# A mixture-of-experts decoder block whose expert weights arrive in 2 MB transfers of 16 KB pieces

## The chip, the cores and the metric

The kernel runs on one core of a Trainium2 chip. The metric is the device time of one execution in microseconds. Three runs of the kernel before took 1349.27, 1349.53 and 1350.82 us; the median is 1349.53 us. The profiled execution took 1348.86 us.

## The reference

The block has a mixing part and an expert part, all in float32, on 256 tokens of width 1024:

```
h = x + hybrid_mixer(rms_norm(x), ...)            # RWKV-7, windowed attention, memory attention, gates
logits = rms_norm(h) @ w_router + b_router        # 32 experts
gates  = softmax(top 4 of logits)
for each expert e, for the tokens that chose it:
    u = xn[tok] @ w1[e] + b1[e]                    # w1[e]: 1024 x 2048, 8 MB
    a = clamped_swiglu(u)                          # u[::2] and u[1::2] -> 1024 columns
    y = a @ w2[e] + b2[e]                          # w2[e]: 1024 x 1024, 4 MB
    h[tok] += gate * y
out = rms_norm(h)
```

All 32 experts are read from HBM once, 12 MB each, 384 MB together. A sum over the contraction rows of w1 (the 1024 columns of xn) or of w2 (the 1024 columns of a) can be taken in any order of the rows, as long as the left factor is laid out in the same order.

## The kernel before, in words

The program has one instruction stream per engine and is synchronised by semaphores. SP issues nearly all DMAs; PE multiplies; DVE and ACT do the pointwise work.

**Mixer part.** 42 chunks of weights of up to 1 MB (`order` in `mixer_chunks`) are loaded through the same ring as the experts' weights. The ring has 16 slots of 8 KB per partition, 1 MB each: slots 0 to 5 lie side by side in `ring`, slots 6 to 15 at the places that `WIDE_AT` lists, in areas that the mixer's own tiles hold before.

**Expert part.** An expert takes 12 chunks: 8 of w1 (128 rows of 2048 columns, one row of 8 KB per partition) and 4 of w2 (256 rows of 1024 columns, two rows of 4 KB per partition, 128 rows apart). The chunks go round the ring in the order w1(0), w1(1), w2(0), w1(2), w2(1), and so on. `load_w1` and `load_w2` (L417 and L425) wait until the chunk that held the slot has been used, `slots_used`, a counter which PE raises once for each chunk; each slot has a semaphore `slot_full` for the landing. Before the w1 of an expert SP also issues two loads of its bias row (L414): 2 partitions by 4 KB each. The first group of experts and the last are written out, those between run in loops.

PE works on pairs of experts (`pair`): `up` of the even expert (8 chunks, 4 matmuls each), `down` of the expert before (4 chunks, 4 matmuls each), `turn` (4 transposes of the activation), `up` of the odd expert with the scatter of the last pair between its chunks, the gather of the next pair's tokens, `down` of the even expert, `turn`. The tokens of an expert sit in 64 places. All of these matmuls stand in the profile as L460, the helper that issues them, each one as two instructions: a chunk is x8.

DVE adds the bias and does the clamped SwiGLU (L1646 to L1659); `act_` is its result, which PE turns into `actT` for `down`. `hn` is the normalised residual (L1586), the left factor of the router and of w1.

Of the kernel before, what the change touches and what calls it, by code (L numbers as in the profile page):

```python
# [16 lines left out]
P = 128  # L17
D = 1024
T = 256
KC = D // P  # L20
# [3 lines left out]
ALU = mybir.AluOpType  # L24
# [7 lines left out]
LEVELS = 6  # L32
# [11 lines left out]
NE = 32  # L44
# [6 lines left out]
RING = 16  # L51
NARROW = 6
SLOT = 2048
CPE = 12
GROUP = 4
TURNS = GROUP * CPE // RING

WIDE_AT = (88, 96, 8, 72, 80, 0, 16, 24, 32, 40)

# [80 lines left out]
def build(nc, x, mem, w_in, rwkv_w2, rwkv_a2, rwkv_g2, swa_sinks, w_mem_kv, w_gate, w_branch, w_out,  # L140
          ffn_norm_w, w_router, b_router, w_exp1, b_exp1, w_exp2, b_exp2, final_norm_w, params, consts, out):
    order, slots = mixer_chunks()
    NMIX = len(order)
# [7 lines left out]
    with ExitStack() as ctx:  # L151
# [10 lines left out]
        xrows = sb("xrows", [P, TT, D])  # L162
# [119 lines left out]
        def slot(s):  # L282
            return ring[:, s * SLOT:(s + 1) * SLOT] if s < NARROW else kb(WIDE_AT[s - NARROW], 8)


        slot_full = [sem(f"slot_full{s}") for s in range(RING)]
# [65 lines left out]
        def _(sp):  # L352
# [7 lines left out]
            for n, (name, c) in enumerate(order):  # L360
                s = slots[n]
                if previous[n] is not None:
                    sp.wait_ge(slots_used, previous[n] + 1)
                elif s == NARROW:
                    sp.wait_ge(pv_sb, 4)
                elif s == NARROW + 2:
                    sp.wait_ge(xx_ps, 2 * (LEVELS - 1))
                elif s == NARROW + 3:
                    sp.wait_ge(y_ps, NCH)
                elif s == NARROW + 5:  # L370
                    sp.wait_ge(y_rwkv_sb, TT)
# [26 lines left out]
            sp.dma_start(b2rows[0:NE, :], b_exp2[0]).then_inc(late_loaded, 16)  # L398
            sp.dma_start(wrt, w_router[0].rearrange("(c p) e -> p c e", p=P)).then_inc(late_loaded, 16)
            sp.dma_start(brt[:], b_router.to_broadcast([P, NE])).then_inc(late_loaded, 16)  # L400

            def load_w1(q, a, r, zero=False, bias=True):

                g = q * (NE // GROUP) + a
                for c in range(KC):
                    s, _, n = w1_place(c, g, r, zero)
                    if c == 0 and bias:
                        sp.wait_ge(b1_spread, g * GROUP + (r - 1))
                        sp.sem_inc(b1_due, 1)
                    sp.wait_ge(slots_used, n + (NMIX - RING + 1))  # L410
                    if c == 0 and bias:
                        for twice in range(2):
                            at = 32 * twice
                            sp.dma_start(b1rows[at:at + 65:64, r % 2, :],  # L414
                                         b_exp1[0, bass.ds(a * GROUP + r, 1), :].rearrange("a (h f) -> (a h) f", h=2))\
                              .then_inc(b1_full[r % 2], 16)
                    sp.dma_start(slot(s), w_exp1[0, bass.ds(a * GROUP + r, 1), c * P:(c + 1) * P, :].rearrange("a p f -> p (a f)"))\  # L417
                      .then_inc(slot_full[s], 16)

            def load_w2(q, a, r, final=False):  # L420
                g = q * (NE // GROUP) + a
                for i in range(4):
                    s, _, n = w2_place(i, g, r, final)
                    sp.wait_ge(slots_used, n + (NMIX - RING + 1))
                    sp.dma_start(slot(s).rearrange("p (c f) -> p c f", c=2),  # L425
                                 w_exp2[0, bass.ds(a * GROUP + r, 1), 2 * i * P:(2 * i + 2) * P, :].rearrange("a (c p) f -> p (a c) f", p=P))\
                      .then_inc(slot_full[s], 16)

# [29 lines left out]
        def _(pe):  # L458
# [407 lines left out]
            for t in range(TT):  # L866
                if t == 1:
                    turn_input(1)
                for c in range(KC):
                    if c % 4 == 0:  # L870
                        pe.wait_ge(hnT_sb, 2 * t + c // 4 + 1)
                    if t == 0 and c == 0:
                        pe.wait_ge(late_loaded, 16 * 5)
                        pe.wait_ge(resid, 1)
# [23 lines left out]
            def up(g, r, E, N, parity, between, zero=False):  # L898

                for c in range(KC):  # L900
                    s, times, n = w1_place(c, g, r, zero)
                    if parity == 0 and c % 4 == 0:
                        pe.wait_ge(xg_sb, N * 2 + c // 4 + 1)
                    pe.wait_ge(slot_full[s], times * 16 + 16 * uses[s])
                    for z in range(2):
# [8 lines left out]

            def down(g, r, E, final=False):

                pe.wait_ge(actT_sb, E + 1)
                for i in range(4):
                    s, times, n = w2_place(i, g, r, final)
                    pe.wait_ge(slot_full[s], times * 16 + 16 * uses[s])  # L920
                    for cc in range(2):
# [46 lines left out]
            def pair(q, a, p, first, last, turn_wait=None):  # L968
# [7 lines left out]
                if not first:  # L976
                    down(g, r - 1, E - 1)
                if very_first:
# [20 lines left out]
                if not last:  # L999
                    gather(N + 1)  # L1000
                down(g, r, E)
                turn(E + 1)

            def one_pass(q, very_first=False):
# [12 lines left out]
                turn_gates(N0 + NPAIR - 1, False)  # L1017
                down(q * (NE // GROUP) + a, GROUP - 1, q * NE + NE - 1, True)
                scatter(N0 + NPAIR - 1, 0)
# [296 lines left out]
        def _(dve):  # L1316
# [259 lines left out]
            for t in range(TT):  # L1576
# [4 lines left out]
                if t == 0:  # L1581
                    dve.wait_ge(late_loaded, 16 * 5)
                link(dve.reciprocal(ss[:, 4 + t:5 + t], ss[:, 4 + t:5 + t]))
                for b in range(2):
                    half = slice(b * 512, (b + 1) * 512)
                    STT(hn[:, t, half], xrows[:, t, half], ss[:, 4 + t:5 + t], ffnw[:, half], ALU.mult, ALU.mult).then_inc(hn_sb, 1)  # L1586

# [53 lines left out]
            def swiglu(E, very_first=False):  # L1641
# [15 lines left out]
                if not very_first:  # L1657
                    dve.wait_ge(actT_ps, E)
                TTn(act_, lin, sig, ALU.mult).then_inc(act_sb, 1)  # L1659

# [90 lines left out]
```

## Time and profile before

| what | value |
|---|---|
| median of three runs | 1349.53 us |
| profiled execution | 1348.86 us |
| its span (first to last instruction) | 1347.1 us |
| PE busy | 1236.4 us, 92% |
| PE weight loads busy | 592.8 us, 44% |
| DVE, ACT busy | 338.3 us, 199.1 us |
| read from HBM | 447.99 MB |
| PE granted clock, mean | 0.987 |

The span starts 1348.86 - 1347.1 = 1.8 us short of the whole time. PE's busy time counts pipelined matmuls up to a modelled end, so that a high share does not say that PE is at its peak; whether PE or a transfer sets the pace has to be read from what PE waits for. The share of the DMA engines can read a little above 1.

### The profile page before, as it was taken

The numbers are of one execution on the slowest core, as the hardware profiler recorded it, in microseconds if no ns is written. First come the engines' busy times: TensorE is split into PE (matmuls) and PEld (weight loads), VectorE is DVE, ScalarE is ACT, GpSimd is POOL, SyncE is SP. The second block draws the span as 40 slices with busy tenths as digits, with TensorE's granted clock in tenths as the row PEclk, the third lists the DMA queues.
The fourth block names the chain that finished last, engine by engine and source line by source line (L and its number), as shares of the span: only waits on it lengthen the run. The fifth ranks groups of instructions, "written<-read, shape, count | busy, mean of one in ns | idle before, by whom it ended". The sixth has DMA issues, their size and how long they took to land.

```text
span 1347.1 us, 16403 instructions
## 1 busy us (share of the span) xinstructions
PE 1236.4 (92%) x6534; PEld 592.8 (44%) x6534; DVE 338.3 (25%) x574; ACT 199.1 (15%) x381; POOL 0.2 (0%) x4
## 2 busy tenths in 40 slices
PE   7999989999989999999998989898998989898985
PEld 6886778888453333333332323232332323232321
DVE  1156463211122123122221212122221212121122
ACT  1225422100111011110111101010110111010112
POOL 0000000000000000000000000000000000000000
PEclk9999989999989999999999999999999999999998
DMA  9343102694549999999999999999999999999992
GB/s 346 110 155 122 64 3 65 225 396 144 206 176 402 417 417 416 417 416 416 417 417 418 418 418 418 417 417 416 418 417 417 418 418 418 416 415 415 413 416 103
DMA packets 95357, 449.72 MB, mean 334 GB/s; under 512 B 8624, under 2 KB 21040, under 8 KB 62544
## 3 DMA queue, kind: packets, MB, share of 16 engines
q1 hardware_dynamic: 95008, 447.99, 83.2%
q10 hardware_dynamic: 304, 1.08, 0.3%
q8 instruction: 34, 0.56, 0.2%
q14 instruction: 11, 0.09, 0.0%
HBM read 447.99 MB, written 1.05 MB: 333 GB/s over the span
## 4 chain that ended last, share of the span: by engine, by line
PE 43%; SPq 32%; DMA 17%; DVE 4%; issue 3%; ACT 1%; ACTq 0%; PEldq 0%; DVEq 0%
PE ps L460 41%; SPq L425 17%; DMA upper<-in_w_exp 9%; SPq L417 7%; DMA ring<-in_w_exp 7%; SPq L414 7%; DVE ring L1381 0%; DVE upper L1472 0%; PE ps L695 0%; SPq L410 0%; DMA xrows<-in_x 0%; PE ps L933 0%; ACT ring L1133 0%; PE ps L476 0%; ACTq L1237 0%
## 5 line engine op out<-in xcount | busy, mean ns | idle before, releaser
L460 PE MATMUL ps<-ring,upper 128*64 128x512 f32 (+4 forms) x2928 | 585.1, 538 | 46.4 <-DMA ring<-in_w_exp 40.5
L460 PEld LDWEIGHTS ps<-ring,upper 128*64 128x64 f32 (+2 forms) x2928 | 176.7, 138 | 405.3 <-issue 289.1
L460 PE MATMUL ps<-upper 128*64 128x512 f32 (+6 forms) x1592 | 278.8, 443 | 24.6 <-DMA upper<-in_w_exp 16.1
L460 PEld LDWEIGHTS ps<-upper 128*64 128x64 f32 (+4 forms) x1592 | 135.1, 162 | 169.7 <-issue 109.3
L460 PE MATMUL ps<-xT,ring 128*128 128x256 f32 x640 | 142.8, 381 | 0.0
L460 PEld LDWEIGHTS ps<-xT,ring 128*128 128x128 f32 x640 | 120.5, 190 | 17.6 <-issue 1.3
L1646 DVE TENSOR_TENSOR upper<-ps,upper 128x512 f32<-128x512 f32 x32 | 22.1, 692 | 364.1 <-PEq L913 364.1
L1666 DVE TENSOR_TENSOR xrows<-xrows,ps 128x1024 f32<-128x1024 f32 x32 | 39.1, 1222 | 264.5 <-PE ps L460 264.5
L1256 ACT ACTIVATE upper<-upper 128x512 f32<-128x512 f32 x32 | 20.2, 631 | 566.1 <-DVE upper L1649 566.1
L1262 ACT ACTIVATE factors<-ps 64x512 f32<-64x512 f32 x64 | 37.9, 593 | 211.8 <-PEq L928 211.1
L460 PE MATMUL ps<-factors,upper 128*128 128x512 f32 x128 | 63.2, 617 | 1.5 <-ACT factors L1262 1.5
L460 PE MATMUL ps<-upper,ring 128*128 128x256 f32 (+1 forms) x304 | 63.5, 367 | 0.0
L460 PEld LDWEIGHTS ps<-upper,ring 128*128 128x128 f32 (+1 forms) x304 | 51.3, 191 | 9.4 <-issue 3.0
L1639 DVE STREAM_SHUFFLE upper<-merged 128x1024 f32<-128x1024 f32 x32 | 42.2, 1320 | 0.2
L460 PEld LDWEIGHTS ps<-factors,upper 128*128 128x128 f32 x128 | 21.8, 189 | 43.7 <-issue 43.7
L933 PEld LDWEIGHTS ps<-cst,upper 128*128 128x128 f32 x128 | 13.7, 143 | 36.7 <-issue 35.1
L933 PE MATMUL ps<-cst,upper 128*128 128x128 f32 x128 | 21.1, 289 | 8.9 <-PE ps L460 8.0
L460 PE MATMUL ps<-xT,upper 128*128 128x256 f32 x128 | 28.3, 379 | 0.0
L460 PE MATMUL ps<-ring,merged 128*128 128x512 f32 x64 | 27.8, 592 | 0.0
L460 PEld LDWEIGHTS ps<-xT,upper 128*128 128x128 f32 x128 | 24.3, 190 | 3.3
L1639 DVE LOAD_MASK_SELECT upper<-merged x32 | 0.4, 14 | 92.6 <-DMA merged<-in_b_exp 92.6
L1510 DVE TENSOR_TENSOR upper<-upper,ps 128x512 f32<-128x512 f32 x8 | 5.5, 688 | 72.3 <-PE ps L460 72.3
(210 smaller groups left out, 499.9 us busy)
## 6 DMA issues: line engine op xcount, KB each, us to landing
ring<-in_w_exp SPq DMA_DIRECT2D x288, 1024.0 KB, 21.4
upper<-in_w_exp SPq DMA_DIRECT2D x96, 1024.0 KB, 22.5
ring<-in_w_gate SPq DMA_DIRECT2D x8, 1024.0 KB, 5.0
ring<-in_w_in SPq DMA_DIRECT2D x8, 896.0 KB, 11.2
ring<-in_w_branch SPq DMA_DIRECT2D x6, 1024.0 KB, 5.3
ring<-in_w_in SPq DMA_DIRECT2D x8, 640.0 KB, 3.9
ring<-in_w_mem_kv SPq DMA_DIRECT2D x4, 1024.0 KB, 4.9
upper<-in_w_gate SPq DMA_DIRECT2D x4, 1024.0 KB, 11.0
```

Of the source, the lines that this page charges most:

```text
L414: sp.dma_start(b1rows[at:at + 65:64, r % 2, :], b_exp1[0, bass.ds(a * GROUP + r, 1), :].rearrange("a (h f) -> (a h) f", h=2))\
L417: sp.dma_start(slot(s), w_exp1[0, bass.ds(a * GROUP + r, 1), c * P:(c + 1) * P, :].rearrange("a p f -> p (a f)"))\
L425: sp.dma_start(slot(s).rearrange("p (c f) -> p c f", c=2), w_exp2[0, bass.ds(a * GROUP + r, 1), 2 * i * P:(2 * i + 2) * P, :].rearrange("a ...
L460: return pe.matmul(o, l, r, start=start, stop=stop, skip_group_check=True)
L933: last = pe.transpose(ps[:, 2, m * P:(m + 1) * P], act_[:, m * P:(m + 1) * P], ident)
L1256: act.activation(sig, glu, ACT.Sigmoid, scale=ALPHA).then_inc(sig_sb, 1)
L1262: act.activation(yrow[64 * parity:64 * parity + 64, dh * 512:(dh + 1) * 512], ps[64 * dh:64 * dh + 64, 3, :], ACT.Copy).then_inc(yrow_sb, 1)
L1510: link(TTn(gsig[:, m % 2, :], gsig[:, m % 2, :], ps[:, 7, :], ALU.mult))
L1639: dve.stream_shuffle(b1all, b1rows[:, parity, :], [0] * 32).then_inc(b1_spread, 1)
L1646: TTn(glu, ps[:, 0, :], b1all[:, 0:D:2], ALU.add).then_inc(glu_raw, 1)
L1666: TTn(a, a, ps[:, bank:bank + 2, :], ALU.add).then_inc(acc_sb, 1)
```

## The change

The contraction rows are permuted within blocks of 512: partition p of a block now holds rows 4p to 4p+3, where it held rows p, p+128, p+256 and p+384. Four neighbouring rows of w2 are then 16 KB in one piece, and so are two neighbouring rows of w1. Two ring slots that lie side by side are filled by one transfer of 2 MB: 128 partitions, one piece of 16 KB each. For w1 the pieces start 32 KB apart (the other two rows of the four belong to the next transfer), for w2 16 KB apart. SP waits until both chunks that held the two slots have been used; PE waits for a landing only at every second chunk. The four last chunks, w2 of expert 31, still come one by one, now in pieces of 8 KB.

The left factors take the same order: `hn` is written with its columns regrouped (which makes router and w1 agree), `act_` likewise for w2; the router's weights come in two DMAs in the same order. `WIDE_AT` is reordered so that slots 6 and 7, 8 and 9, ... are neighbours; with that the mixer's chunks in slots 8 to 11 lie in other places and two waits of the mixer's loads move.

```diff
-WIDE_AT = (88, 96, 8, 72, 80, 0, 16, 24, 32, 40)
+WIDE_AT = (88, 96, 72, 80, 0, 8, 16, 24, 32, 40)
...
+        def twin_slot(s):
+            return ring[:, s * SLOT:(s + 2) * SLOT] if s < NARROW else kb(WIDE_AT[s - NARROW], 16)
...
                 elif s == NARROW + 2:
-                    sp.wait_ge(xx_ps, 2 * (LEVELS - 1))
-                elif s == NARROW + 3:
                     sp.wait_ge(y_ps, NCH)
-                elif s == NARROW + 5:
+                elif s == NARROW + 6:
                     sp.wait_ge(y_rwkv_sb, TT)
...
-            sp.dma_start(wrt, w_router[0].rearrange("(c p) e -> p c e", p=P)).then_inc(late_loaded, 16)
+            for b in range(2):
+                sp.dma_start(wrt[:, 4 * b:4 * b + 4, :], w_router[0, b * 512:(b + 1) * 512, :].rearrange("(p c) e -> p c e", c=4)).then_inc(late_loaded, 16)
...
-                for c in range(KC):
+                for c in range(0, KC, 2):
                     s, _, n = w1_place(c, g, r, zero)
...
-                    sp.wait_ge(slots_used, n + (NMIX - RING + 1))
+                    sp.wait_ge(slots_used, n + (NMIX - RING + 2))
...
-                    sp.dma_start(slot(s), w_exp1[0, bass.ds(a * GROUP + r, 1), c * P:(c + 1) * P, :].rearrange("a p f -> p (a f)"))\
+                    b, j = c // 4, c % 4
+                    sp.dma_start(twin_slot(s), w_exp1[0, bass.ds(a * GROUP + r, 1), b * 512:(b + 1) * 512, :]
+                                 .rearrange("a (p c) f -> p a c f", c=4)[:, :, j:j + 2, :].rearrange("p a c f -> p (a c f)"))\
...
-                for i in range(4):
+                for i in range(0, 4, 1 if final else 2):
                     s, _, n = w2_place(i, g, r, final)
...
+                    if final:
+                        sp.dma_start(slot(s), src[:, :, j:j + 2, :].rearrange("p a c f -> p (a c f)")).then_inc(slot_full[s], 16)
+                    else:
+                        sp.dma_start(twin_slot(s), src.rearrange("p a c f -> p (a c f)")).then_inc(slot_full[s], 16)
...
             def up(g, r, E, N, parity, between, zero=False):
-                    pe.wait_ge(slot_full[s], times * 16 + 16 * uses[s])
+                    if c % 2 == 0:
+                        pe.wait_ge(slot_full[s], times * 16 + 16 * uses[s])
...
-                    STT(hn[:, t, half], xrows[:, t, half], ss[:, 4 + t:5 + t], ffnw[:, half], ALU.mult, ALU.mult).then_inc(hn_sb, 1)
+                    STT(hn[:, t, half].rearrange("p (c q) -> p q c", c=4), xrows[:, t, half].rearrange("p (q c) -> p q c", c=4),
+                        ss[:, 4 + t:5 + t], ffnw[:, half].rearrange("p (q c) -> p q c", c=4), ALU.mult, ALU.mult).then_inc(hn_sb, 1)
...
-                TTn(act_, lin, sig, ALU.mult).then_inc(act_sb, 1)
+                TTn(act_.rearrange("p (c q) -> p q c", c=4), lin.rearrange("p (q c) -> p q c", c=4), sig.rearrange("p (q c) -> p q c", c=4),
+                    ALU.mult).then_inc(act_sb, 1)
```

On SP, where the mixer's last loads have been issued and the experts' begin, 6 + 2 + 1 + 2 + 5 loads of w1 and four of w2 stood before (L417 is w1, L425 w2; 128x2048 is one row of 8 KB per partition):

```order
L417 DMA ring<-in_w_exp 128x2048 [waits slots_used] x6
L417 DMA upper<-in_w_exp 128x2048 [waits slots_used] x2
L417 DMA ring<-in_w_exp 128x2048 [waits slots_used]
L417 DMA upper<-in_w_exp 128x2048 [waits slots_used] x2
L417 DMA ring<-in_w_exp 128x2048 [waits slots_used] x5
L425 DMA ring<-in_w_exp 128x2x1024 [waits slots_used] x4
```

The same stretch of SP after the change (L420 is w1, L434 w2):

```order
L420 DMA ring<-in_w_exp 128x4096 [waits slots_used] x3
L420 DMA upper<-in_w_exp 128x4096 [waits slots_used] x2
L420 DMA ring<-in_w_exp 128x4096 [waits slots_used] x3
L434 DMA ring<-in_w_exp 128x4096 [waits slots_used] x2
```

Half as many loads stand there, each of 4096 elements per partition, and each waits for two chunks instead of one.

On PE, near the end, `down` of expert 30 stood before as four chunks with a wait for a landing each:

```order
L460 MATMUL ps<-ring,upper 64x512 [waits slots_used,slot_full8,actT_sb]
L460 MATMUL ps<-ring,upper 64x512 x3
L460 MATMUL ps<-upper 64x512 [waits slot_full9]
L460 MATMUL ps<-upper 64x512 x3
L460 MATMUL ps<-upper 64x512 [waits slot_full10]
L460 MATMUL ps<-upper 64x512 x3
L460 MATMUL ps<-ring,upper 64x512 [waits slot_full11]
L460 MATMUL ps<-ring,upper 64x512 x3
```

The same stretch of PE now:

```order
L467 MATMUL ps<-upper 64x512 [waits slots_used,slot_full8,actT_sb]
L467 MATMUL ps<-upper 64x512 x7
L467 MATMUL ps<-ring,upper 64x512 [waits slot_full10]
L467 MATMUL ps<-ring,upper 64x512 x7
```

The first of two chunks can start only when both have landed; `down` of expert 31 behind it keeps its four waits.

## Rows read from the trace of the kernel before

**Rows 1.** The page's 40 slices of the span: DMA share in tenths, and GB/s

```profile
DMA  9343102694549999999999999999999999999992
GB/s 346 110 155 122 64 3 65 225 396 144 206 176 402 417 417 416 417 416 416 417 417 418 418 418 418 417 417 416 418 417 417 418 418 418 416 415 415 413 416 103
```

**Rows 2.** Timeline of SP's queue: start us, us, issues; two bias loads, four experts apart

```profile
1025.51 5.11 SPq L414 DMA_DIRECT2D merged<-in_b_exp  x2
...
1147.78 5.11 SPq L414 DMA_DIRECT2D merged<-in_b_exp  x2
```

**Rows 3.** Timeline of PE, one up and down: start us, us, instructions, idle before

```profile
1086.96 2.02 PE L460 MATMUL ps<-ring,upper 128*64 128x512 f32 x8 [0.46 <-DMA ring<-in_w_exp]
1089.44 2.02 PE L460 MATMUL ps<-ring,upper 128*64 128x512 f32 x8 [0.46 <-DMA ring<-in_w_exp]
1091.92 2.02 PE L460 MATMUL ps<-ring,upper 128*64 128x512 f32 x8 [0.46 <-DMA ring<-in_w_exp]
1094.46 2.02 PE L460 MATMUL ps<-ring,upper 128*64 128x512 f32 x8 [0.52 <-DMA ring<-in_w_exp]
1097.03 1.94 PE L460 MATMUL ps<-ring,upper 128*64 128x512 f32 x8 [0.54 <-DMA ring<-in_w_exp]
1099.59 1.94 PE L460 MATMUL ps<-ring,upper 128*64 128x512 f32 x8 [0.62 <-DMA ring<-in_w_exp]
1102.15 1.94 PE L460 MATMUL ps<-upper 128*64 128x512 f32 x8 [0.63 <-DMA upper<-in_w_exp]
1104.76 1.94 PE L460 MATMUL ps<-upper 128*64 128x512 f32 x8 [0.67 <-DMA upper<-in_w_exp]
```

**Rows 4.** Busy time by stretch: stretch us, PE, PEld, DVE, ACT, POOL, clock, DMA share, GB/s

```profile
640.00:701.10 61.10, 55.71 (x251) 19.23 (x251) 13.83 (x24) 6.30 (x11) 0.00 (x0) 1.00 1.02 417
...
1026.00:1034.00 8.00, 6.70 (x28) 1.78 (x30) 0.00 (x0) 0.00 (x0) 0.00 (x0) 1.00 1.02 411
1044.00:1054.00 10.00, 9.12 (x40) 2.71 (x37) 1.33 (x2) 2.16 (x4) 0.00 (x0) 1.00 1.01 423
```

**Rows 5.** The page's DMA packets, and its queues: packets, MB, share

```profile
DMA packets 95357, 449.72 MB, mean 334 GB/s; under 512 B 8624, under 2 KB 21040, under 8 KB 62544
...
q8 instruction: 34, 0.56, 0.2%
```

**Rows 6.** Timeline where the experts begin: SP's last prefetch, PE's first chunks, SP's restart

```profile
366.50 0.33 SPq L417 DMA_DIRECT2D ring<-in_w_exp  x1
...
386.08 4.27 PE L460 MATMUL ps<-ring,upper 128*64 128x512 f32 x18 [0.69 <-ACT upper L1252]
...
388.14 2.18 SPq L425 DMA_DIRECT2D ring<-in_w_exp  x2
```

**Rows 7.** Busy time by stretch, after the restart

```profile
388.00:440.00 52.00, 50.30 (x228) 18.60 (x226) 12.65 (x21) 6.38 (x10) 0.00 (x0) 0.97 0.98 389
```

**Rows 8.** Busy time by stretch, at the end of the transfers

```profile
1318.00:1322.00 4.00, 2.78 (x14) 1.12 (x14) 0.00 (x0) 1.42 (x3) 0.00 (x0) 1.00 0.24 96
1322.00:1326.00 4.00, 3.59 (x18) 1.23 (x20) 0.00 (x0) 2.12 (x4) 0.00 (x0) 1.00 0.12 50
```

**Rows 9.** Timeline of PE at the end

```profile
1318.45 1.94 PE L460 MATMUL ps<-ring,upper 128*64 128x512 f32 x8 [0.58 <-DMA ring<-in_w_exp]
...
1322.41 5.37 PE L460 MATMUL ps<-ring,upper 128*64 128x512 f32 x24 [1.02 <-ACT upper L1267]
...
1328.33 1.94 PE L460 MATMUL ps<-ring,upper 128*64 128x512 f32 x8 [0.55 <-DMA ring<-in_w_exp]
```

**Rows 10.** DVE's two changed instructions: ns min/median/max, first and last start us

```profile
L1586 DVE SCALAR_TENSOR_TENSOR upper<-xrows,ss,xT x4: 744/748/752, 356.0 to 370.0; 128x512 f32<-128x512 f32 x4
...
L1659 DVE TENSOR_TENSOR upper<-upper x32: 691/692/693, 403.7 to 1313.8; 128x512 f32<-128x512 f32 x32
```

**Rows 11.** Busy time by stretch: the input projection's weights, 7 KB pieces 12 KB apart

```profile
16.00:20.00 4.00, 4.00 (x20) 3.54 (x19) 1.22 (x3) 2.48 (x5) 0.00 (x0) 1.00 1.04 385
...
24.00:30.00 6.00, 6.00 (x29) 5.30 (x28) 0.00 (x0) 0.00 (x0) 0.00 (x0) 1.00 1.02 417
```

More of the change, by code:

```diff
@@ L421, in load_w2 @@
                 g = q * (NE // GROUP) + a
-                for i in range(4):
+                for i in range(0, 4, 1 if final else 2):
                     s, _, n = w2_place(i, g, r, final)
[L424 to L427, printed above, removed]
+                    sp.wait_ge(slots_used, n + (NMIX - RING + (1 if final else 2)))
+                    b, j = i // 2, 2 * (i % 2)
+                    src = w_exp2[0, bass.ds(a * GROUP + r, 1), b * 512:(b + 1) * 512, :].rearrange("a (p c) f -> p a c f", c=4)
+                    if final:
+                        sp.dma_start(slot(s), src[:, :, j:j + 2, :].rearrange("p a c f -> p (a c f)")).then_inc(slot_full[s], 16)
+                    else:
+                        sp.dma_start(twin_slot(s), src.rearrange("p a c f -> p (a c f)")).then_inc(slot_full[s], 16)
             def load_group(q, a, count=GROUP, bias_from=0):
@@ L872, in _ @@
                     if t == 0 and c == 0:
-                        pe.wait_ge(late_loaded, 16 * 5)
+                        pe.wait_ge(late_loaded, 16 * 6)
                         pe.wait_ge(resid, 1)
@@ L913, in up, with down @@
                 pe.sem_inc(up_ps, 1)
-            def down(g, r, E, final=False):
+            def down(q, g, r, E, final=False):
                 pe.wait_ge(actT_sb, E + 1)
@@ L919, in down @@
                     s, times, n = w2_place(i, g, r, final)
-                    pe.wait_ge(slot_full[s], times * 16 + 16 * uses[s])
+                    if i % 2 == 0:
+                        pe.wait_ge(slot_full[s], times * 16 + 16 * uses[s])
+                    elif final:
+                        pe.wait_ge(slot_full[s], q * 16 + 16 * (uses[s] + 1))
                     for cc in range(2):
@@ L976, in pair @@
                 if not first:
-                    down(g, r - 1, E - 1)
+                    down(q, g, r - 1, E - 1)
                 if very_first:
@@ L1000, in pair @@
                     gather(N + 1)
-                down(g, r, E)
+                down(q, g, r, E)
                 turn(E + 1)
@@ L1017, in one_pass @@
                 turn_gates(N0 + NPAIR - 1, False)
-                down(q * (NE // GROUP) + a, GROUP - 1, q * NE + NE - 1, True)
+                down(q, q * (NE // GROUP) + a, GROUP - 1, q * NE + NE - 1, True)
                 scatter(N0 + NPAIR - 1, 0)
@@ L1581, in _ @@
                 if t == 0:
-                    dve.wait_ge(late_loaded, 16 * 5)
+                    dve.wait_ge(late_loaded, 16 * 6)
                 link(dve.reciprocal(ss[:, 4 + t:5 + t], ss[:, 4 + t:5 + t]))
```

## The prediction

> **What bounds the kernel now.** I began with the page's slices [rows 1]. From the twelfth of 40 on the DMA engines are busy nearly all the time and move 402 to 418 GB/s; only the last slice falls off. That is the expert part, some 940 of the 1347 us. PE reads 9 in most of these slices too, so the slices alone do not decide. The first row of the stretches, one pair of experts, does [rows 4]: 61.10 us, of which PE is busy 55.71, with the clock at 1.00, so 5.4 us a pair are left over, and the DMA share is 1.02. What ends PE's idle time stands in its timeline [rows 3]: each chunk of eight instructions takes 2 us and is preceded by half a microsecond of waiting for a DMA into ring or upper. PE follows the landings one by one. The period of an expert is read from SP's bias loads, which come once each: (1147.78 - 1025.51) / 4 = 30.57 us [rows 2].
>
> The same rows say what a landing costs. While w1 lands (8 KB pieces) the steps are 2.48, 2.48 and 2.54 us, mean 2.50; while w2 lands (4 KB pieces) they are (1104.76 - 1094.46) / 4 = 2.575 us [rows 3]. Eight of the one and four of the other make 30.3 us; the 0.27 us to the period are the two bias loads, whose four 4 KB pieces lie on two partitions and so on few engines.
>
> That the pace is set by the engines with the most work, not by the mean rate, is seen at the end: the traffic falls to 96 GB/s between 1318 and 1322 us and 50 between 1322 and 1326 [rows 8], while PE still waits for a landing at 1328.33 [rows 9]. Most engines are done ten microseconds before the last. Thirty experts with 0.27 to 0.3 us more on a few engines make just about that lead. So I count with PE's landing steps, not with the 417 GB/s.
>
> **The pieces.** 128 pieces over 16 engines are 8 each for a w1 chunk, 256 are 16 each for a w2 chunk; the bytes are equal. Eight pieces more cost 2.575 - 2.50 = 0.075 us, which is 9.4 ns a piece. The mean rates agree: 423 GB/s in a stretch of 8 KB pieces and 411 in one of 4 KB [rows 4] are 2.48 and 2.55 us for 1 MB. Two w1 chunks take 5.00 us with 16 pieces an engine; in one transfer with 8 pieces they take 5.00 - 0.075 = 4.925 us, and two w2 chunks the same, instead of 5.15. This assumes that a 16 KB piece travels as one. The trace has packets of that size: 34 on the instruction queue with 0.56 MB together, 16.5 KB each [rows 5]. And the 8 KB pieces are not cut: 95357 packets less the 62544 under 8 KB leave 32813, where w1 alone makes 32 x 8 x 128 = 32768.
>
> The sum: 16 of the 384 chunks are in the ring before PE begins. From the restart at 388.14 us [rows 6] 240 chunks of w1 and 128 of w2 follow: 240 x 2.50 + 128 x 2.575 + 30 x 0.27 = 937.7 us; the trace has 1328.33 - 388.14 = 940.2, the rest being the first landing's delay. After: 182 transfers x 4.925 + 4 single chunks x 2.50 + 30 x 0.27 = 914.5 us. That is -23.2 us.
>
> The bounds: the closest steps (2.54 and 2.56) give 2.5 ns a piece, a transfer of 4.98 us and -13 us; the farthest (2.48 and 2.61) give 16 ns, 4.83 us and -41 us. I take the means, which the rates bear out.
>
> **The coarser ring.** Three costs.
> At the restart the first transfer needs two used chunks. SP's queue stood still between 366.50 and 388.14, when PE had used the first [rows 6]; PE goes at 4.27 us for 18 instructions, 1.9 us for the eight of a chunk. The restart moves back by 1.9 us, and since the transfers set the end from there, all of it counts. Behind it, DMA is just kept fed for a while (389 GB/s between 388 and 440 us, [rows 7]); releases in pairs add a bit of idle, which I put at 0.4 us: four transfers end some 20 us after the restart, just where PE has come through the first two chunks of the second expert. Bounds 0 and 2.
> Later PE needs (61.10 - 5.4) / 2 = 27.9 us for an expert and the transfers 29.8, so DMA remains the slower side. Of eight double slots one or two are with PE and six are ordered ahead; nothing starves.
> At the end PE used the last chunk of expert 30 from 1318.45 on, and began expert 31's `down` at 1322.41, 4.0 us later (two of matmuls, two of transposes and evictions) [rows 9]. Now both last chunks of expert 30 land together, four single landings (9.9 us) before the last. PE needs 3.9 us for them, 2.0 for the transposes, and 5.37 / 3 = 1.8 us for each of four chunks: 13.1 us, so it ends 3.2 us after the last landing, where it ended 1.94 after it. +1.3 us, with PE the bound there; bounds 0 and 2.
> Together +3.6 us.
>
> **What is put at nothing.** DVE's 32 writes of `act_` (0.69 us each, [rows 10]) now go in four interleaved columns; a doubled time would hide, since DVE waits most of an expert's 30 us and even the last one ends at 1314.5, six microseconds before PE transposes it. The four writes of `hn` are different: PE waits for them before the router. Two lie on the path; equal elements, so I take 0, with twice their 0.75 us, +1.5, as the upper bound. SP issues half as many loads and stands in its queue anyway. The router's second DMA is issued during the mixer. The mixer's loads that change place wait for things that the neighbouring load already waited for, and the queue did not stand there.
>
> Sum: -23.2 + 3.6 = -19.6 us against the profiled 1348.86: 1329.3. The median of the runs is 0.7 above the profiled one, so 1330.0.
>
> **Rivals.**
> A, the pieces are cut at 8 KB. Then w1 gains nothing and w2 0.075 us a chunk: 128 x 0.075 = -9.6 us, with the costs of the ring -6.0: 1343.5. Against it: packets of 16 KB exist; for it: those belong to another queue and none of a load is above 8 KB. The Trainium skill (DMA: Bandwidth & Descriptors, SWDGE vs HWDGE vs iDMA) says a packet has preferably at most 4096 bytes, for descriptors written by software; by that rule 4 and 8 KB pieces would cost the same and the change would be left with its costs, +3.6 us or 1353. The trace disagrees, with its 32813 packets of 8 KB or more.
> B, slower: w1's pieces now start 32 KB apart and the engines read from places 128 KB apart, instead of through one unbroken megabyte; if HBM serves that worse, each w1 transfer pays. The nearest rows read 7 KB pieces 12 KB apart: 417 GB/s in one stretch, 385 in another, where small loads are mixed in [rows 11]. If 401, the middle of these, were due to the steps, a w1 transfer would take 5.00 x 422 / 401 = 5.26 us, 0.335 more than counted, and 120 of them +40: about 1370. The gain is gone when a w1 transfer takes 19.6 / 120 = 0.16 us more than 4.925, that is from 5.09 us. Against it: 417 is what pieces of that size would give in any place. The Trainium skill (DMA: Bandwidth & Descriptors, Latency and other measured facts) has copies at a row step of 512 KB almost at full rate and at 2 MB and above down to three quarters and half; no run here shows such steps, and 32 KB is far below, so it adds no chance.
> C, the ring's costs eat the gain: pieces cost 2.5 ns only, and the upper bounds of the ring (1.9 + 2 + 2 + 1.5) hold: -13 + 7.4, 1344.
> D, the pieces cost more than the means say, at 16 ns: -41 + 3.6, 1312.
>
> **Chances.** Forecast 0.65, A 0.12, B 0.12, C 0.06, D 0.05. The range that holds eight in ten is 1317 to 1345: it reaches most of the way to D and includes A and C, and leaves out B. A difference below 0.2%, 2.7 us, can hardly be told from none. Faster 0.85, same 0.04, slower 0.11.
>
> **What would show it.** SP's bias loads in the profile after should come every 29.8 us (30.2 under A, over 30.6 under B); PE should wait for a DMA at every second chunk of eight, with steps of 4.93 us in both w1 and w2; the mean rate should be near 427 GB/s; the page should count some 40,700 packets fewer in all (65,536 of the experts' weights become 190 x 128 + 4 x 128 = 24,832) and about as many of 8 KB or more as that last number. The first expert load after the prefetch should be issued at about 390.0 us, and PE should run 13 us without a wait at the end. Equal steps for w1 and w2 at 5.0 would speak for A; w1's above w2's for B. A restart much later than 390 us, or idle DMA in the middle of the loop, would show that I have the ring wrong.

## The result and the profile after

The changed kernel takes 1331.72 us (median of four runs, 1330.19 to 1332.04) against 1350.09 before on the same chip: ratio 0.9862, interval 0.9845 to 0.9879, or 18.4 us faster. Forecast were 1330.0 and a range of 1317 to 1345. Run again beside later kernels it gave 1331.72 once more. Its profiled execution has a span of 1328.8 us, 18.3 less than before.

The page's slices, which answer to [rows 1], show the same plateau, higher and shorter:

```profile
DMA  9343101694449999999999999999999999999991
GB/s 347 106 163 127 64 3 62 200 395 177 158 158 400 417 427 428 428 426 428 429 428 429 427 428 428 428 428 427 429 428 428 427 428 428 428 428 427 427 424 71
DMA packets 50861, 449.70 MB, mean 338 GB/s; under 512 B 4577, under 2 KB 17249, under 8 KB 25985
```

428 GB/s stand where 417 stood. Of 8 KB or more there are 50861 - 25985 = 24876 packets, and 24832 were forecast: the 16 KB pieces travel whole. Cut at 8 KB they would be twice as many. In all 44,500 packets are gone, not 40,700, since the small packets fell too (under 512 B: 8624 to 4577).

SP's timeline, start us, us, issues, at the bias loads, against [rows 2]:

```profile
1029.88 1.11 SPq L416 DMA_DIRECT2D merged<-in_b_exp  x2
...
1149.33 1.11 SPq L416 DMA_DIRECT2D merged<-in_b_exp  x2
```

Four experts in 119.45 us: the period is 29.86 us, 0.71 less than 30.57 (forecast 29.82).

PE's timeline in the loop, against [rows 3]:

```profile
1080.80 3.82 PE L467 MATMUL ps<-ring,upper 128*64 128x512 f32 x16 [1.07 <-DMA ring<-in_w_exp]
1085.69 3.65 PE L467 MATMUL ps<-ring,upper 128*64 128x512 f32 x16 [1.07 <-DMA ring<-in_w_exp]
1090.63 3.65 PE L467 MATMUL ps<-upper 128*64 128x512 f32 x16 [1.28 <-DMA upper<-in_w_exp]
...
1135.69 3.82 PE L467 MATMUL ps<-upper 128*64 128x512 f32 x16 [0.23 <-DMA upper<-in_w_exp]
1140.51 3.82 PE L467 MATMUL ps<-ring,upper 128*64 128x512 f32 x16 [0.99 <-DMA ring<-in_w_exp]
```

PE now takes two chunks at a landing and waits a microsecond for the next. The first two steps end in landings of w2 (the rows of 3.65 us) and are 4.89 and 4.94 us; the last ends in one of w1 (3.82 us) and is 4.82 us. Forecast was 4.93 for both.

Where the transfers start again after the prefetch (against [rows 6, 7]), SP's timeline, and then the busy time by stretch, whose last two columns are DMA share and GB/s:

```profile
389.76 3.93 SPq L434 DMA_DIRECT2D ring<-in_w_exp  x2
```

```profile
388.00:440.00 52.00, 49.96 (x224) 18.40 (x222) 13.38 (x21) 6.38 (x10) 0.00 (x0) 0.97 0.93 374
```

The restart is at 389.76 us (forecast 390.0, before 388.14), and 374 GB/s instead of 389 move until 440.

PE's timeline at the end (against [rows 9]):

```profile
1295.45 3.65 PE L467 MATMUL ps<-upper 128*64 128x512 f32 x16 [0.31 <-PE ps L467]
1299.58 3.65 PE L467 MATMUL ps<-ring,upper 128*64 128x512 f32 x16 [0.47 <-DMA ring<-in_w_exp]
...
1305.25 7.09 PE L467 MATMUL ps<-ring,upper 128*64 128x512 f32 x32 [1.02 <-ACT upper L1278]
```

The last wait for a landing is 0.47 us at 1299.58; the four chunks of expert 31 run through in 7.09 us without one. PE ends them at 1312.34 where it ended at 1330.27. But PE was nearly without waits before that, too: of what it waited for between 1274 and 1313 us, the profile's waits (engine and line, waited for, us, times, longest) give

```profile
PE ps L467 <- DMA ring<-in_w_exp: 1.9, 3, 1.0
```

One thing was put at nothing and is not. The changed lines of DVE, against [rows 10], each from its own line's view:

```profile
L1671 DVE TENSOR_TENSOR upper<-upper x32: 1034/1064/1078, 403.5 to 1298.0; 128x512 f32<-128x512 f32 x32
```

```profile
L1597 DVE SCALAR_TENSOR_TENSOR upper<-xrows,ss,xT x4: 1094/1094/1108, 355.2 to 369.5; 128x512 f32<-128x512 f32 x4
```

Writing the 512 elements in four interleaved columns takes 1.06 and 1.09 us instead of 0.69 and 0.75.

### The profile page after: what moved, and what is told of

It reads as the page before. It is cut to its first block, busy times and chain, and to the rows that moved or that the text cites. A ratio compares the mean times of both kernels' runs of the same rounds, so it can differ in the third digit from the quotient of the medians.

```text
span 1328.8 us, 15782 instructions
## 1 busy us (share of the span) xinstructions
PE 1222.1 (92%) x6534; PEld 599.7 (45%) x6534; DVE 350.4 (26%) x574; ACT 199.0 (15%) x381; POOL 0.2 (0%) x4
## 2 busy tenths in 40 slices
DMA packets 50861, 449.70 MB, mean 338 GB/s; under 512 B 4577, under 2 KB 17249, under 8 KB 25985
## 4 chain that ended last, share of the span: by engine, by line
PE 62%; DMA 30%; DVE 4%; ACT 1%; issue 1%; SPq 0%; PEldq 0%; DVEq 0%
PE ps L467 61%; DMA ring<-in_w_exp 30%; DVE ring L1392 0%; PE ps L944 0%; DVE upper L1483 0%; PE ps L702 0%; DMA xrows<-in_x 0%; ACT ring L1144 0%; PE ps L483 0%; ACT factors L1273 0%; DVE upper L1597 0%; PE ps L852 0%; PE ps L611 0%; DVE ring L1389 0%; ACT ring L1170 0%
## 5 line engine op out<-in xcount | busy, mean ns | idle before, releaser
L467 PE MATMUL ps<-ring,upper 128*64 128x512 f32 (+4 forms) x2928 | 572.4, 534 | 45.5 <-DMA ring<-in_w_exp 41.1
L467 PE MATMUL ps<-upper 128*64 128x512 f32 (+6 forms) x1624 | 283.4, 442 | 20.9 <-DMA upper<-in_w_exp 12.2
L467 PEld LDWEIGHTS ps<-upper 128*64 128x64 f32 (+3 forms) x1624 | 144.3, 163 | 151.7 <-issue 132.6
L467 PE MATMUL ps<-xT,ring 128*128 128x256 f32 x672 | 150.0, 381 | 0.0
L467 PEld LDWEIGHTS ps<-xT,ring 128*128 128x128 f32 x672 | 126.7, 190 | 18.4 <-issue 1.3
L467 PE MATMUL ps<-upper,ring 128*128 128x256 f32 (+1 forms) x272 | 56.6, 368 | 0.0
L467 PEld LDWEIGHTS ps<-upper,ring 128*128 128x128 f32 (+1 forms) x272 | 45.5, 192 | 8.7 <-issue 3.0
L467 PEld LDWEIGHTS ps<-factors,upper 128*128 128x128 f32 x128 | 21.8, 189 | 43.7 <-issue 43.7
L1671 DVE TENSOR_TENSOR upper<-upper 128x512 f32<-128x512 f32 x32 | 34.1, 1064 | 1.2 <-ACT upper L1267 0.2
L1263 ACT ACTIVATE upper<-ps 128x512 f32<-128x512 f32 x32 | 17.4, 595 | 34.5 <-PE ps L467 34.5
L1666 DVE SCALAR_TENSOR_TENSOR upper<-upper 128x512 f32<-128x512 f32 x32 | 22.2, 693 | 1.1
## 6 DMA issues: line engine op xcount, KB each, us to landing
ring<-in_w_out SPq DMA_DIRECT2D x4, 1024.0 KB, 14.3
```

The costliest lines, as they stand in the source:

```text
L467: return pe.matmul(o, l, r, start=start, stop=stop, skip_group_check=True)
L1263: act.activation(xg[:, 4 * b:4 * b + 4, :], ps[:, 4 + b, :].rearrange("p (c s) -> p c s", c=4), ACT.Copy).then_inc(xg_sb, 1)
L1666: STT(lin, lin, 1.0, glu, ALU.add, ALU.mult).then_inc(prod_sb, 1)
L1671: TTn(act_.rearrange("p (c q) -> p q c", c=4), lin.rearrange("p (q c) -> p q c", c=4), sig.rearrange("p (q c) -> p q c", c=4), ALU.mult).t ...
```

## The experiments

### Pieces of 8 KB, single slots, permuted rows

```diff
-                for c in range(0, KC, 2):
+                for c in range(KC):
...
-                    sp.wait_ge(slots_used, n + (NMIX - RING + 2))
+                    sp.wait_ge(slots_used, n + (NMIX - RING + 1))
...
-                    sp.dma_start(twin_slot(s), ...[:, :, j:j + 2, :]...)
+                    sp.dma_start(slot(s), ...[:, :, j:j + 1, :]...)
```

(w2 likewise as four loads, and PE waits at each chunk.)

> Rows permuted as in the changed kernel, but each slot filled by its own 1 MB transfer with one 8 KB piece per partition: w1 in 8 KB pieces 32 KB apart, w2 in 8 KB pieces instead of 4 KB, 16 single slots. My theory (a piece costs about 9.4 ns beyond its bytes, their distance nothing): w1 lands every 2.50 us as before, w2 every 2.50 instead of 2.575, so 128 chunks x 0.075 = 9.6 us less than before, no cost of a coarser ring, some 1 us for the wider writes of DVE on the way to the experts: 0.994 of before, 1341 us. Rival 1 (the size of a transfer brings the gain, not the piece): no change, 1350. Rival 2 (pieces 32 KB apart are read more slowly, and the 16 KB pieces only hide that): w1 above 2.50 us, 1350 or more.

1343.25 us, ratio 0.9952 (0.9939 to 0.9966): 6.6 us less than before (1349.85 beside it), where 8.6 were expected. Transfers are as large as before, so their size is not what brings these 6.6 us; rival 1 falls. The timeline of PE, in w1 and after it in w2:

```profile
1083.68 2.02 PE L467 MATMUL ps<-ring,upper 128*64 128x512 f32 x8 [0.42 <-DMA ring<-in_w_exp]
1086.16 2.02 PE L467 MATMUL ps<-ring,upper 128*64 128x512 f32 x8 [0.46 <-DMA ring<-in_w_exp]
...
1096.09 1.94 PE L467 MATMUL ps<-ring,upper 128*64 128x512 f32 x8 [0.54 <-DMA ring<-in_w_exp]
1098.57 1.94 PE L467 MATMUL ps<-upper 128*64 128x512 f32 x8 [0.54 <-DMA upper<-in_w_exp]
```

Both land every 2.48 us. w1's pieces now lie 32 KB apart and cost what they cost side by side; rival 2 falls, and with it rival B of the prediction. The expert's period is (1137.12 - 1015.99) / 4 = 30.28 us by SP's bias loads. That is 0.29 less than before, 8.9 us over the 30.67 experts (368 chunks) that land after the restart; why only 6.6 came of it is not shown.

### Double slots with the old rows, and each layer alone: a square of four

The changed kernel with both, one or none of the layers in the new row order; rings, waits and 2 MB transfers the same. Old rows in w1 read

```diff
-                    sp.dma_start(twin_slot(s), w_exp1[...b * 512:(b + 1) * 512, :]
-                                 .rearrange("a (p c) f -> p a c f", c=4)[:, :, j:j + 2, :]...)
+                    sp.dma_start(twin_slot(s).rearrange("p (c f) -> p c f", c=2),
+                                 w_exp1[...c * P:(c + 2) * P, :].rearrange("a (c p) f -> p (a c) f", p=P))
```

> 2 MB transfers into double slots, but the rows in their old order: w1 in 8 KB pieces, w2 in 4 KB pieces, so the piece count of before with the transfers and the ring of after. My theory: the landings cost as before (5.00 and 5.15 us per 2 MB), and only the ring's costs show, 1.9 us at the restart, up to 2 of idle DMA behind it, 1.3 at the end: 3.6 to 5 us slower than before, 1.003. Rival (a transfer has a cost of its own, so fewer of them bring the gain): as fast as the changed kernel, 0.986.

> 2 MB transfers into double slots; only w2 in the new row order with 16 KB pieces, w1 in its old order with two 8 KB pieces. My theory: against the kernel with old rows and double slots, 62 transfers land in 4.925 instead of 5.15 us and four chunks in 2.50 instead of 2.575: 14.3 us less, so some 10 us faster than before, 0.9925. If pieces cost nothing beyond 8 KB, 62 x 0.15 = 9.6 us less.

> 2 MB transfers into double slots; only w1 in the new row order with 16 KB pieces, w2 in its old order with four 4 KB pieces. My theory: against the kernel with old rows and double slots, 120 transfers land in 4.925 instead of 5.00 us: 9 us less, some 5 us faster than before, 0.996. The gains of this and of the kernel with w2 alone should add up to that of the changed kernel over the one with old rows and double slots. If pieces cost nothing beyond 8 KB: no difference to old rows with double slots.

| double slots, 2 MB transfers | median us | ratio to before (interval) | expert's period us |
|---|---|---|---|
| old rows in both (8 KB and 4 KB) | 1352.50 | 1.0019 (1.0010 to 1.0028) | 30.54 |
| w1 in 16 KB pieces | 1344.45 | 0.9959 (0.9946 to 0.9973) | 30.24 |
| w2 in 16 KB pieces | 1339.81 | 0.9927 (0.9914 to 0.9941) | 30.15 |
| both (the changed kernel) | 1331.72 | 0.9862 (0.9845 to 0.9879) | 29.86 |

Larger transfers alone are 2.6 us slower. The rows of w1 bring 8.1 us and those of w2 12.7, together 20.8; from 1352.50 to 1331.72 it is 20.8. They add up; that they do so to a tenth is luck, since the runs of the w1 kernel alone lie between 1342.61 and 1345.53. So within a microsecond or two nothing but the number of pieces is needed to tell the story. The forecasts of the two were 9 and 14.3.

One rival stands in no forecast: SP's own queue. Before the change the issue of two bias loads took 5.11 us [rows 2], after it 1.11, and SP's queue has a large share of the chain of work that ended last. The chain by engine, from the pages of the kernel before, of the one with w2 alone in 16 KB pieces, and of the changed kernel:

```profile
PE 43%; SPq 32%; DMA 17%; DVE 4%; issue 3%; ACT 1%; ACTq 0%; PEldq 0%; DVEq 0%
...
PE 60%; DMA 33%; DVE 4%; ACT 1%; issue 1%; ACTq 0%; SPq 0%; PEldq 0%; DVEq 0%
...
PE 62%; DMA 30%; DVE 4%; ACT 1%; issue 1%; SPq 0%; PEldq 0%; DVEq 0%
```

SP's queue is out of the chain in the second kernel already, and yet it is 8.1 us slower than the changed kernel. So w1's share of the gain is not SP's. For w2's share there is no such pair of runs; against SP as the limit speaks that the DMA engines had work all the time before, with a share of 1.01 to 1.02 [rows 4], and that a piece costs nearly the same in both layers: by the periods (30.54 - 30.24) / 32 = 9.4 ns for w1, which has 32 pieces an engine fewer, and (30.54 - 30.15) / 48 = 8.1 ns for w2, which has 48 fewer.

### Bias pieces of 32 bytes

```diff
-                            sp.dma_start(b1rows[at:at + 65:64, r % 2, :],
-                                         b_exp1[...].rearrange("a (h f) -> (a h) f", h=2))
+                            sp.dma_start(b1rows[at:at + 65:64, r % 2, 0:8],
+                                         b_exp1[...].rearrange("a (h f) -> (a h) f", h=2)[:, 0:8])
```

> The changed kernel, whose bias loads of experts 2 to 31 bring only the first 8 numbers of each half (pieces of 32 bytes instead of 4 KB); the rest of their bias row is left as it was. My theory: the pace is that of the few DMA engines that carry the bias pieces beside their share of the weights; with those gone the period of an expert falls from 29.87 us to that of the others, about 0.3 us less, 30 experts 8 to 9 us: 1323, and the last traffic of all engines ends within 2 us instead of trailing for 10. Rival (the mean rate of 428 GB/s is the bound, the trailing engines are a harmless end effect): 8 KB less an expert is 0.02 us, no change, 1331.

1321.69 us, ratio 0.9786 (0.9773 to 0.9799): 10.0 us less than the changed kernel, with a plateau of 428 GB/s as there. It leaves out most of 30 bias rows, so it serves to measure only. The busy time by stretch (DMA share and GB/s at the end of a row) at the end of the transfers, the changed kernel first:

```profile
1284.00:1296.00 12.00, 11.69 (x48) 3.51 (x48) 3.13 (x4) 0.00 (x0) 0.00 (x0) 1.00 0.99 415
1296.00:1300.00 4.00, 3.53 (x18) 1.14 (x16) 3.68 (x7) 0.63 (x1) 0.00 (x0) 1.00 0.39 164
1300.00:1304.00 4.00, 3.84 (x22) 1.50 (x18) 0.00 (x0) 0.60 (x2) 0.00 (x0) 1.00 0.19 78
1304.00:1308.00 4.00, 2.98 (x17) 1.04 (x16) 0.00 (x0) 2.94 (x5) 0.00 (x0) 1.00 0.07 29
1308.00:1309.00 1.00, 1.00 (x8) 0.31 (x6) 0.00 (x0) 0.00 (x0) 0.00 (x0) 1.00 0.04 16
```

and with short bias pieces:

```profile
1284.00:1296.00 12.00, 10.45 (x50) 3.41 (x46) 4.39 (x8) 1.48 (x3) 0.00 (x0) 1.00 1.01 424
1296.00:1300.00 4.00, 2.99 (x14) 1.06 (x16) 0.00 (x0) 2.69 (x5) 0.00 (x0) 1.00 0.64 268
1300.00:1304.00 4.00, 4.00 (x20) 1.15 (x16) 0.00 (x0) 0.00 (x0) 0.00 (x0) 1.00 0.01 4
```

Without the bias pieces all engines end together; with them a few trail for ten microseconds: a share of 0.19 is about three engines of 16, one of 0.07 about one. The expert's period is (1142.47 - 1025.05) / 4 = 29.36 us: 16 KB of bias pieces an expert, a thousandth of its bytes, cost 0.51 us of 29.86. The prediction had 0.27.

Thirty experts at 0.51 would make 15.3 us, and the time fell by 10.0. SP's bias loads, in the changed kernel and then in this one, show why the rest is missing:

```profile
431.00 1.03 SPq L416 DMA_DIRECT2D merged<-in_b_exp  x2
...
647.35 1.11 SPq L416 DMA_DIRECT2D merged<-in_b_exp  x2
```

```profile
433.00 1.03 SPq L416 DMA_DIRECT2D merged<-in_b_exp  x2
...
649.46 0.52 SPq L416 DMA_DIRECT2D merged<-in_b_exp  x1
```

Eight experts take 216.35 and 216.46 us, 27.05 us each, and in neither kernel does PE wait for a DMA in that stretch. PE lives on the full ring there and sets the pace, and the bias pieces cost nothing. Only the 20 or so experts after it pay, at 0.51 us each.

This puts the landing steps right, if the bias pieces cost 0.51 us in the other kernels too, which was measured in the changed one alone. Less 0.51, an expert's period is 30.06 before, 29.77 in the first experiment and 29.35 after. The first experiment has only 8 KB pieces: 29.77 / 12 = 2.481 us for 1 MB. Then w2's 4 KB pieces took (30.06 - 8 x 2.481) / 4 = 2.553 and the 16 KB pieces take 29.35 / 12 = 2.446. Eight pieces less on an engine save 0.072 us from 4 to 8 KB; from 8 to 16 KB four less save 0.035 us. Both are 9 ns a piece. The differences of the periods need no term for the bias and say the same: (30.57 - 30.28) / 32 = 9.1 ns and (30.28 - 29.86) / 48 = 8.8 ns.

### DVE writes in unbroken order

```diff
-                    STT(hn[:, t, half].rearrange("p (c q) -> p q c", c=4), xrows[:, t, half].rearrange(...),
+                    STT(hn[:, t, half], xrows[:, t, half], ss[:, 4 + t:5 + t], ffnw[:, half], ALU.mult, ALU.mult)
...
-                TTn(act_.rearrange("p (c q) -> p q c", c=4), lin.rearrange(...), sig.rearrange(...), ALU.mult)
+                TTn(act_, lin, sig, ALU.mult)
```

> The changed kernel with DVE's writes of hn and act_ in unbroken order as before, so that the left factors do not fit the order of the weights' rows (the products are of permuted rows; all sizes and all work are the same). My theory: the writes in four interleaved columns took 1064 and 1016 ns instead of 692 and 706, and of that only the two halves of hn in front of the router and the first expert's act_ are waited for: 0.9 to 1.4 us less than the changed kernel, 1330.5. Rival (none of it is on the path): no difference, 1331.7.

1330.57 us, 1.2 less than the changed kernel, where 0.9 to 1.4 were expected. The ranges of the two overlap (1329.96 to 1331.46 here, 1330.19 to 1332.87 in the changed kernel's eight runs), so neither the size nor the gain is proven. The profile does not show it either: PE's first chunk of the experts starts at 386.01 us here, and at 385.90 and 386.17 in the two profiled executions of the changed kernel. The rival stands. (The left factors do not fit the weights' rows here, so this kernel does not compute the reference.)

### Single transfers at the restart and at the end

```diff
-                for i in range(0, 4, 1 if final else 2):
+                for i in range(0, 4, 1 if split else 2):
```

(with `split` for w2 of experts 0 and 30, and the waits to match.)

> The changed kernel, in which w2 of expert 0 (the first loads after PE has begun) and w2 of expert 30 come in four single transfers of 1 MB with 8 KB pieces, each with its own wait. My theory: the restart comes one chunk, 1.9 us, sooner, and at the end PE gets the third of the last six chunks sooner, 1.3 us; four more pairs of pieces cost 0.3 us: 2.5 to 3 us less than the changed kernel, 1329. Rival (the early idle time is set by PE's pace of release alone, so what the restart wins is lost again before 440 us): only the end counts, 1330.5.

1331.43 us, 0.3 less: my theory of the two ends falls. PE's timeline at the end of this kernel:

```profile
1292.07 3.82 PE L467 MATMUL ps<-upper 128*64 128x512 f32 x16
1296.21 3.65 PE L467 MATMUL ps<-upper 128*64 128x512 f32 x16 [0.32 <-PE ps L467]
1299.66 3.63 PE L467 MATMUL ps<-ring,upper 128*64 128x512 f32 x16
...
1305.31 7.09 PE L467 MATMUL ps<-ring,upper 128*64 128x512 f32 x32 [1.02 <-ACT upper L1278]
```

The wait of 0.47 us is gone, and PE's last wait for a landing comes before its chunk at 1280.74: PE's own work fills the last thirty microseconds, so there was no more to win here. At the other end the restart came at 388.84 us, though PE began 0.9 us later than in the changed kernel (386.78 against 385.90), and yet only 369 GB/s moved up to 440, against 374. That fits the rival, by which PE's releases bound the transfers there, however early they start. From PE's first chunk on, the restart came 2.06 us later here and 3.86 in the changed kernel; the bias load at 1150.12 us here and the same one at 1149.33 there come 763.34 and 763.43 us later. Of the 1.8 us won at the restart 0.1 is left.

### Bias loads from GpSimd

```diff
+        @block.gpsimd
+        def _(pool):
+            def bias(q, a, r, free=False):
+                if not free:
+                    pool.wait_ge(b1_spread, (q * (NE // GROUP) + a) * GROUP + (r - 1))
+                for twice in range(2):
+                    at = 32 * twice
+                    pool.dma_start(b1rows[at:at + 65:64, r % 2, :], b_exp1[...]).then_inc(b1_full[r % 2], 16)
```

> The changed kernel with all expert bias loads issued by GpSimd instead of SP and ACT, unchanged in size and target, one expert ahead of need. My theory: if that queue puts its pieces on other engines from load to load, the extra 0.3 us an expert is shared by all 16 and the time falls by up to 7 us, to 1325. If it uses the same few engines each time, the time stays at 1331 to 1332; if the pieces come too late for DVE, PE waits for the activation and it is slower.

1327.66 us, ratio 0.9825 (0.9812 to 0.9838): 4.1 us less than the changed kernel, and the fastest here that computes the reference. Its bias loads stand in the timeline of POOL at

```profile
1032.23 1.07 POOL L472 DMA_DIRECT2D merged<-in_b_exp  x2 [25.45 <-DVE upper L1669]
...
1151.07 1.07 POOL L472 DMA_DIRECT2D merged<-in_b_exp  x2 [25.45 <-DVE upper L1669]
```

which is a period of 29.71 us, between 29.36 and 29.86. Of the 0.51 us a third is saved. Which engines took the pieces was not seen; that the traffic at the end falls more steeply (240 GB/s from 1300 to 1304 us, 47 to 1308) fits a wider share. So do the packets: the page's queues, with packets, MB and share, have

```profile
q1 hardware_dynamic: 50272, 447.48, 81.7%
q10 hardware_dynamic: 288, 1.05, 0.2%
q0 software_dynamic: 2048, 0.53, 0.2%
```

The 64 bias loads are 32 packets each on GpSimd's queue, where they were 4 each on SP's and ACT's (256 packets fewer stand there). 1791 more of all packets are under 2 KB, so most of the new ones are small and the 4 KB pieces are still whole. How much of the 4.1 us comes from the bias is open: 20 experts at 0.15 us give 3.0. In the profiled execution, the slowest of the five, PE's last chunk ended only 0.5 us earlier than in the changed kernel, and the output's store was issued 0.5 us earlier; the other 1.7 us of the span lay behind that.

### Bias loads of one partition each

```diff
-                        for twice in range(2):
-                            at = 32 * twice
-                            sp.dma_start(b1rows[at:at + 65:64, r % 2, :], ...)
+                        for quarter in range(4):
+                            at, h = 32 * quarter, quarter // 2
+                            sp.dma_start(b1rows[at:at + 1, r % 2, :].rearrange("p (k f) -> p k f", k=16), ...)
```

> The changed kernel, whose bias row comes in four loads of one partition each (4 KB, given as 16 runs of 64 numbers) instead of two loads of two partitions; same bytes, same issuing queue. My theory: the run with shortened bias pieces took 0.51 us off an expert's period, since the bias pieces lie on the few engines that set the pace. If a load of one partition is dealt out over all 16 engines, in pieces of 256 bytes, the engines share it and most of the 10 us of that run come back: 1323 to 1325. Rival (a load of one partition goes to one engine whole): that engine has 4 pieces an expert, the time rises by 5 to 15 us.

> The kernel before (old rows, 1 MB transfers) with the bias loads of one partition each. My theory: the cost of the bias on the pacing engines is the same there, so it gains what the changed kernel gains by the same edit, within 2 us. Rival (the trailing engines mattered only in the changed kernel): no change, 1350.

> Both the bias loads of one partition each and w2 of experts 0 and 30 in four single transfers. With the bias spread the end is nearer to PE's own pace, so the split ends bring at most what they brought alone: 0 to 1 us less than the kernel with the bias spread alone.

The rival was right, and my theory fell: 1341.42 us, 9.7 more than the changed kernel run beside it (1331.72). In the kernel before the same edit costs 8.9 us (1358.25, ratio 1.0064, 1.0050 to 1.0077): the same within 2 us, as was expected, but a loss and no gain. So the few loaded engines set the pace there as well. With the split ends the changed kernel with this edit takes 1341.19, no difference. The end of the transfers of the first of these kernels, by stretch:

```profile
1308.00:1312.00 4.00, 3.64 (x18) 1.23 (x16) 3.90 (x8) 0.63 (x1) 0.00 (x0) 1.00 0.06 27
1312.00:1316.00 4.00, 3.84 (x21) 1.38 (x18) 0.01 (x1) 0.50 (x1) 0.00 (x0) 1.00 0.06 27
1316.00:1320.00 4.00, 2.98 (x16) 1.04 (x16) 0.00 (x0) 3.04 (x6) 0.00 (x0) 1.00 0.06 27
```

For twelve microseconds and more 27 GB/s move, a sixteenth of 428: one engine's worth, and the share of 0.06 says the same. That this engine has all four pieces of each bias row is the rival's reading; it fits, though the trace does not name engines. The page counts 50860 packets, 4576 of them under 512 B, where it counted 50861 and 4577, so the 16 runs of a load were not cut apart. The period is (1159.98 - 1039.30) / 4 = 30.17 us, 0.82 above the kernel with short bias pieces.

The changed kernel again, for these comparisons:

> The changed kernel once more, beside the others on the same chip: 1331 to 1332 us, against which the small differences of the other kernels are read.

1331.72 us, 1330.49 to 1332.87.

## Why the prediction was right, step by step

**The bound** was named rightly: the landings on the slowest engines. The two bias experiments show it in both directions, with 10.0 us less and 9.7 us more at the same mean rate of 428 GB/s. It holds from about 650 us on; before that PE works off the full ring at 27.05 us an expert without a wait for a DMA. The prediction left that stretch out.

**The cost of a piece** was put at 9.4 ns and is 9.0. The term that was mis-sized is the bias: 0.27 us an expert by subtraction of the mean landing steps, 0.51 when it is taken away. (Its four pieces also lie on four partitions, two to a load, and not on two.) The steps of 2.54 and 2.61 us in [rows 3] are longer than the others around them, and I averaged them in. With 2.48 and 2.553 the gain of an expert is 30.57 - 29.86 = 0.71 us, over 30.67 experts 21.8, where the prediction had 23.2. The square of four has 20.8. In the profile the last bytes move between 1308 and 1309 us, some 919 us after the restart at 389.76, where it was 940 before: 21 us less.

**The ring's costs** were put at +3.6 us and are 2.6 (old rows, double slots). The delays themselves stand in the profile about as forecast: the restart comes 1.6 us later (1.9 forecast), and PE ends 3 to 4 us after the last bytes where it ended 1.9 after the last landing (3.2 forecast). What failed is that they count. The prediction says of the restart's delay that all of it counts, but taking it away left 0.1 us by 1150 us; and taking the last pair of expert 30 apart won next to nothing, since PE had its own work to do from 1281 us on. Both together won 0.3 us instead of 2.5. So the sum came out near by luck, and what makes up the 2.6 us is open.

**DVE's writes** were put at nothing, with +1.5 as the bound. They take half as long again. Whether any of it is on the path is not shown: the kernel without them is 1.2 us faster, within the spread of the runs. The last write of `act_` ends at 1299.1 us and PE transposes it at 1303.4, so it hides as forecast.

The sum with measured terms: -20.8 + 2.6 = -18.2 against -18.4 measured; DVE's writes are in these two numbers already, since each layer's rows bring its own writes. That these agree within the spread of the runs is no separate proof: the two terms are differences of the same medians. The prediction's -19.6 was 1.2 too good, 2.4 in the landings and 1.0 the other way in the ring.

**The rivals.** A (pieces cut at 8 KB) falls by the packet count and by w1 alone, which brought 8.1 us. That 4 and 8 KB pieces cost the same falls by the first experiment, whose period is 0.29 us shorter. B (pieces 32 KB apart are slower) falls by the single-slot kernel's 2.48 us. C and D stand on 2.5 and 16 ns a piece, and it is 9. C's price was also worked out wrongly: with the steps it names, 2.54 and 2.56 us, a w1 transfer goes from 5.08 to 5.06 us and a w2 transfer from 5.12 to 5.06, which makes -6 us and not -13, and with its ring C would have been about 1351, outside the range.

## What to carry to other kernels

Where PE follows the landings of a full ring, count the pieces per DMA engine, since each costs about 9 ns here beside its bytes; a permutation of contraction rows that is free in the sum can halve them. Then look at how the traffic ends: if it trails off instead of stopping, some engines carry more than others, and a small load on few partitions in every round can cost far more than its share of the bytes (here 1.7% of the period where landings set the pace, and 10 us of 1332 in all, for a thousandth of them). Larger transfers by themselves brought nothing here and cost 2.6 us; that this comes of the coarser ring is argued, not shown.

## What the runs showed of the hardware that was not expected

- Two loads of two partitions with 4 KB pieces, 16 KB in all, cost 0.51 us an expert; as four loads of one partition they cost 0.82 us, with a tail at a sixteenth of the full rate. Writing such a load as 16 runs of 64 numbers did not spread it; the runs lie end to end, and the number of packets did not change.
- A DVE instruction of 512 elements that writes them in four columns 512 bytes apart took 1.06 us instead of 0.69.
- The price of a piece was about the same 9 ns from 4 to 8 KB and from 8 to 16 KB, also when the pieces lay 32 KB apart.
